# Latent attention of a two-block transformer kernel: units of one head or of two

## Chip, cores and metric

One core of a Trainium2 chip. The metric is the time of one execution on the device in microseconds (us).

## The reference, cut to what matters

The program computes two blocks of two layers each on 512 tokens of width 1024 (and 256 context tokens in the first block). The change lies in the second layer of the first block, in its latent attention: four heads, each with a nope part of 128 dimensions and a rotated part of 64; the rotated key is one for all heads. 512 queries attend to 768 keys (512 tokens and 256 of context), with values of 128 dimensions a head:

```python
q_nope, q_pe = q[..., :C_NOPE_DIM], q[..., C_NOPE_DIM:]      # 128 and 64
k_nope, v = kv[..., :C_NOPE_DIM], kv[..., C_NOPE_DIM:]       # 128 and 128
q = jnp.concatenate([q_nope, q_pe], axis=-1)
k = jnp.concatenate([k_nope, jnp.broadcast_to(k_pe, (B, T, C_HEADS, C_ROPE_DIM))], axis=-1)
...
s = jnp.einsum('bqhd,bkhd->bhqk', q, k).astype(jnp.float32) * (q.shape[-1] ** -0.5)
p = jax.nn.softmax(s, axis=-1).astype(v.dtype)
return jnp.einsum('bhqk,bkhe->bqhe', p, v)
```

## The kernel before, in words

The whole program is one kernel with five instruction streams, one for each engine, written out in program order; semaphores order them against each other. There are six attention stages (A, B in the first layer; M, the latent one, and N in the second; S and D in the second block), and all go through the same functions. All matrices of the attention are float32, and a float32 matmul shows as two records in the trace.

**Units and turns.** `units_m` (L612) makes the work of stage M as units: one head and 128 queries, so 4 heads x 4 = 16 units. `seated` (L508) puts them into turns, here one unit a turn, and gives each its places: the PSUM banks of its scores (L519), the column of its probabilities in SBUF, and its blocks of 128 keys, in groups of four, for the transposes.

```python
U["sb"] = [0, 2] if wide_s and nh == 2 else [alt, 2 + alt] if nh == 2 else [2 * alt]
```

`wide_s` is true for over 512 keys: the scores of a head then take two banks. A single head of 768 keys stands in banks 0 and 1 or in 2 and 3, by turns (`alt`). Two heads of 768 keys, as in stages B and N, take banks 0 to 3 in every turn.

**One step of the stage** (`attention`, L1146 for PE, L1875 for ACT, L2583 for DVE): in step i PE makes the scores of turn i, then the transposes ("flips") of the probabilities of turn i - 2 (`LAG`, L538), then the value products of turn i - 3. In the same step DVE takes the maxima of turn i (`maxima`, L2510: a reduce over 768 columns in PSUM and a small negation for each head) and divides the probabilities of turn i - 1 by their sum (`weigh`, L2543). ACT copies the first two groups of transposes of turn i - 2 to SBUF, makes the first exp of turn i (`exps`, L1845, which reads the scores in PSUM), copies the third group if there is one, and makes the second exp if there is one.

**Banks.** `take_bank` (L889) makes PE wait, before it writes to a bank, until the last reader has emptied it: for scores without a mask that is the exp. In `scores` (L1064) it is called for the banks of all heads of the unit before the first matmul. `next_bank` (L877) goes round a set of banks; for the transposes of stage M that set is banks 4 and 5 (`FLIP_BANKS`, L736: `"M": [4, 5], "N": [4, 5, 7]`), and such a bank is emptied by ACT's copy. The outputs of stage M stand in bank 6 (even heads) and 7 (odd heads), and `take_out` (L2604) multiplies them with their gate on DVE when a head's four units are done.

**Rotated part.** Two heads share one tile of rotated queries: one on partitions 0 to 63, one on 64 to 127; the rotated keys stand on both halves. A unit of one head uses all 128 rows in both its matmuls: POOL copies the rotated queries of the head into a buffer whose other half is zero (`QZ_at`, L533, three places in `EXQ`; the copies at L3353 to L3362), and PE waits for that copy before the rotated matmul. In stages B and N a unit is a pair of heads, and each head's matmul uses 64 rows of the array.

**Modulation steps.** The scale, shift and gate vectors of later layers are made beside everything else, in steps (`ada_step`: L903, L1758, L2365, L3185, L3514), which all engines count alike: a "chunk" (DVE multiplies a loaded 128x1024 piece by the condition, two instructions), a "sum", and an "apply" (PE transposes or multiplies the sums; DVE or ACT takes the result). A group is four chunks, a sum and an apply. `ada(n)` makes up to n steps and ends early at a "sum". `STEP_TURNS` (L289) says after which steps of stage M one such call is made: 18 calls. SyncE issues the load of a piece when DVE is done with the piece two before it (`NADA`, L18).

The projections ahead of stage M and behind it are matmuls on PE; the one behind it starts without a barrier on PE.

Of the kernel before, what the change touches and what calls it, by code (L numbers as in the profile page):

```python
# [288 lines left out]
STEP_TURNS = {"M": range(18)}  # L289
# [8 lines left out]
def program(nc, A, out_d):  # L298
    ctx = ExitStack()
    with ctx:  # L300
# [232 lines left out]
        def QZ_at(u, hf):  # L533
            return EXQ[:, u % 3 * 256 + hf * 128:u % 3 * 256 + hf * 128 + 128]

# [74 lines left out]
        def units_m():  # L612
            units = []
            for h in range(4):
                ob = 6 + h % 2
                for n in range(4):
                    heads = [[(k0, w, [(qn(h, n * 128, n * 128 + 128), kn(h, k0, k0 + w)), (None, kr(k0, k0 + w))])
                              for k0, w in ((0, 512), (512, 256))]]
                    pv = [(0, z * 128, 128, Bg(vm + z * 512 + h * 128, vm + z * 512 + (h + 1) * 128),
                           bank(ob, n * 128, n * 128 + 128)) for z in range(6)]  # L620
                    units.append(dict(heads=heads, halves=[h % 2],
                                      q=[half(qr(h // 2, n * 128, n * 128 + 128), h % 2)],
                                      nk=768, masks=[None], scale=192.0 ** -0.5, pv=pv, ob=ob, first=True, last=True,
                                      done=(h, 0, 512) if n == 3 else None))
            return seated([[U] for U in units], "M")
# [246 lines left out]
        def tensor(pe):  # L872
# [191 lines left out]
            def scores(tag, u, U):  # L1064
# [9 lines left out]
                for z in range(len(U["heads"][0])):  # L1074
                    for h in range(nh):
                        col, w, pairs = U["heads"][h][z]
                        at = U["sb"][h] * 512 + col
                        for j, (l, r) in enumerate(pairs):
                            if l is None and nh == 1:
                                pe.wait_ge(pool_value, ("qz", tag, u))  # L1080
                                l = QZ_at(u, U["halves"][h])
                            elif l is None:
                                l, r = U["q"][h], half(r, U["halves"][h])
                            pe.matmul(PS[:, at:at + w], l, r, j == 0, j == len(pairs) - 1)
                        if z == len(U["heads"][0]) - 1:
                            pe.then_inc(pe_scores, ("scores", tag, u, h))
# [15 lines left out]
            def products(tag, u, U):  # L1102
# [5 lines left out]
                if U["first"]:  # L1108
                    take_bank(U["ob"], [])
# [2732 lines left out]
```

## Time and profile before

| | |
|---|---|
| Median of 3 runs | 2261.98 us |
| The three runs | 2262.75, 2252.33, 2261.98 us |
| The profiled execution | 2252.27 us |
| Its span in the profile | 2250.5 us |
| Mean granted clock of TensorE | 0.995 |
| TensorE busy | 2187.8 us |
| VectorE busy | 1260.9 us |
| ScalarE busy | 841.0 us |
| GpSimd busy | 345.8 us |

Times in the rows are microseconds from the start of the span. A timeline row gives start and length, the engine (PE is TensorE's matmuls, PEld its weight loads, DVE VectorE, ACT ScalarE, POOL GpSimd, SP SyncE), the line of the kernel, the instruction with output and inputs, how many instructions are merged in the row, and in brackets how long the engine was idle before it and who released it. Most lines named are those of small helpers that record every instruction, so the tiles tell more than the line. The ends of matmuls are modelled and overlap the next one's start; starts are the better guide. The granted clock is a share of 2.4 GHz.

### The profile page before, as it was taken

The numbers are of one execution on the slowest core, as the hardware profiler recorded it, in microseconds if no ns is written. First come the engines' busy times: TensorE is split into PE (matmuls) and PEld (weight loads), VectorE is DVE, ScalarE is ACT, GpSimd is POOL, SyncE is SP. The second block draws the span as 40 slices with busy tenths as digits, with TensorE's granted clock in tenths as the row PEclk, the third lists the DMA queues.
The fourth block names the chain that finished last, engine by engine and source line by source line (L and its number), as shares of the span: only waits on it lengthen the run. The fifth ranks groups of instructions, "written<-read, shape, count | busy, mean of one in ns | idle before, by whom it ended". The sixth has DMA issues, their size and how long they took to land.

```text
span 2250.5 us, 30697 instructions
## 1 busy us (share of the span) xinstructions
PE 2187.8 (97%) x12072; PEld 1726.4 (77%) x12072; DVE 1260.9 (56%) x2566; ACT 841.0 (37%) x1763; POOL 345.8 (15%) x342
## 2 busy tenths in 40 slices
PE   7999999999999999999999999999999999999998
PEld 4877886688547576788777988887778688888886
DVE  3666666763346436578666565562468836433334
ACT  4366424521123105533475322223533733222243
POOL 2300211000000102030100100004533001000144
PEclk9999999999999999999999999999999999999999
DMA  8201340013233452032210455553222104322231
GB/s 322 85 20 39 111 142 1 19 57 108 84 131 104 127 177 76 11 127 93 94 39 2 140 195 189 185 188 114 88 91 78 36 1 142 129 103 94 94 107 71
DMA packets 58268, 225.85 MB, mean 100 GB/s; under 512 B 20478, under 2 KB 21118, under 8 KB 41740
## 3 DMA queue, kind: packets, MB, share of 16 engines
q1 hardware_dynamic: 58124, 223.88, 29.1%
q8 instruction: 96, 1.57, 0.3%
q14 instruction: 48, 0.39, 0.1%
HBM read 221.76 MB, written 2.10 MB: 99 GB/s over the span
## 4 chain that ended last, share of the span: by engine, by line
PE 84%; DVE 6%; ACT 2%; POOL 2%; issue 1%; DMA 0%; POOLq 0%; DVEq 0%; ACTq 0%
PE PS L86 79%; PE PS L91 5%; POOL WKr L103 1%; ACT WK L98 1%; DVE ACC L115 1%; DVE WK L108 1%; ACT WK L96 1%; ACT WKr L96 1%; DVE SM L135 0%; DVE RINGr L103 0%; DVE WK L142 0%; DVE WK L115 0%; ACT GB L96 0%; DVE X L115 0%; DVE WK L103 0%
## 5 line engine op out<-in xcount | busy, mean ns | idle before, releaser
L86 PE MATMUL PS<-Hr,RINGr 128*128 128x512 f32 (+1 forms) x1304 | 474.1, 368 | 0.0
L86 PE MATMUL PS<-Hr,GBr 128*128 128x512 f32 (+2 forms) x1396 | 462.9, 382 | 0.2 <-DVE GB L115 0.2
L96 ACT ACTIVATE WK<-PS 128x512 f32<-128x512 f32 (+3 forms) x367 | 186.0, 541 | 396.1 <-PE PS L86 224.4
L86 PEld LDWEIGHTS PS<-Hr,GBr 128*128 128x128 f32 (+1 forms) x1396 | 259.8, 188 | 52.6 <-issue 4.1
L86 PEld LDWEIGHTS PS<-Hr,RINGr 128*128 128x128 f32 x1304 | 244.8, 188 | 41.6
L103 DVE TENSOR_TENSOR RINGr<-RING,GBr 128x1024 fp32r<-128x1024 f32 x148 | 184.0, 1281 | 140.7 <-ACT GBr L96 139.9
L86 PE MATMUL PS<-RING,GB 128*128 128x256 f32 x1152 | 251.1, 379 | 0.0
L86 PEld LDWEIGHTS PS<-RING,GB 128*128 128x128 f32 x1152 | 218.2, 190 | 31.2 <-issue 2.1
L115 DVE SCALAR_TENSOR_TENSOR ACC<-ADA,SM,ACC 128x512 f32<-128x512 f32 x280 | 214.7, 788 | 47.8 <-DMA ADA<-in_l_mod 35.1
L86 PE MATMUL PS<-GBr,WKr 128*128 128x512 f32 (+1 forms) x748 | 238.4, 381 | 2.8 <-POOL WKr L103 2.8
L96 ACT ACTIVATE GBr<-RING 128x1024 fp32r<-128x1024 f32 x158 | 158.2, 1046 | 189.4 <-PE PS L86 189.4
L86 PE MATMUL PS<-H,RING 128*128 128x512 f32 (+1 forms) x544 | 204.7, 530 | 1.4 <-DVE GB L115 1.4
L96 ACT ACTIVATE GB<-PS 32x512 f32<-32x512 f32 (+3 forms) x152 | 81.0, 533 | 259.3 <-PE PS L86 253.7
L86 PE MATMUL PS<-GB 64*128 64x256 f32 (+5 forms) x976 | 166.8, 436 | 10.2 <-ACT WK L98 4.6
L86 PE MATMUL PS<-Xr,GBr 128*128 128x512 f32 (+2 forms) x484 | 175.3, 376 | 0.0
L86 PEld LDWEIGHTS PS<-H,RING 128*128 128x128 f32 x544 | 101.3, 190 | 88.4 <-issue 82.7
L86 PEld LDWEIGHTS PS<-GBr,WKr 128*128 128x128 f32 x748 | 140.6, 188 | 35.6 <-issue 7.2
L91 PE MATMUL PS<-CN,WK 128*128 128x128 f32 x1104 | 149.1, 278 | 17.4 <-DVE WK L108 9.9
L91 PEld LDWEIGHTS PS<-CN,WK 128*128 128x128 f32 x1104 | 120.6, 140 | 58.3 <-issue 40.2
L103 POOL TENSOR_TENSOR WKr<-GB,WKr 128x512 fp32r<-128x512 f32 x76 | 109.4, 1440 | 339.1 <-ACT WKr L96 336.2
L86 PE MATMUL PS<-WK,GB 128*64 128x128 f32 (+1 forms) x1856 | 148.1, 278 | 1.3 <-DVE GB L115 0.8
L98 ACT ACTIVATE WK<-WK,SM 128x128 f32<-128x128 f32 (+5 forms) x224 | 135.4, 612 | 21.3 <-DVE SM L142 13.2
(236 smaller groups left out, 3014.7 us busy)
## 6 DMA issues: line engine op xcount, KB each, us to landing
ADA<-in_l_mod SPq DMA_DIRECT2D x96, 512.0 KB, 4.2
RING<-in_l_gu SPq DMA_DIRECT2D x44, 1024.0 KB, 4.9
RING<-in_l_wd SPq DMA_DIRECT2D x24, 1024.0 KB, 5.0
RING<-in_ev_in SPq DMA_DIRECT2D x13, 1024.0 KB, 5.9
ADA<-in_od_ada SPq DMA_DIRECT2D x24, 512.0 KB, 3.7
RING<-in_od_in SPq DMA_DIRECT2D x11, 1024.0 KB, 5.9
RING<-in_l_in SPq DMA_DIRECT2D x10, 1024.0 KB, 5.0
RING<-in_l_out SPq DMA_DIRECT2D x8, 1024.0 KB, 4.9
```

What stands on the lines that cost most here:

```text
L86: self.last = self.eng.matmul(out, lhsT, rhs, start=start, stop=stop, skip_group_check=True)
L91: self.last = self.eng.transpose(out, in_, ident)
L96: self.last = self.eng.activation(out, in_, func, bias=bias, scale=scale)
L98: self.last = self.eng.activation(out, in_, func, bias=bias, scale=scale, accum_out=accum)
L103: self.last = self.eng.tensor_tensor(out, a, b, op)
L108: self.last = self.eng.tensor_scalar(out, a, s1, None, op0)
L115: self.last = self.eng.scalar_tensor_tensor(out=out, in0=a, scalar=s, in1=b, op0=op0, op1=op1)
```

## The change

A unit of stage M becomes two heads and 128 queries: eight units and eight turns. For each piece of keys PE makes the nope matmuls of both heads, then the two rotated matmuls, each on its own half of 64 rows and into its head's banks. The zero-widened queries go, with POOL's copies and its memset of their buffer. A unit's 12 blocks of keys make three groups of transposes. The outputs of both heads are taken together, in banks 6 and 7, and taken out one after the other on DVE when the pair's four units are done. The modulation calls of the stage become nine calls of up to two steps. The bank set of the transposes stays as it is. The diff:

```diff
--- before.py
+++ after.py
@@ -286,7 +286,7 @@
 
 
 
-STEP_TURNS = {"M": range(18)}
+STEP_TURNS = {"M": range(9)}
 FFN_STEPS = {"l0f": 3, "l1f": 1}
 OUT_STEPS = (3, 2, 1, 0)
 
@@ -529,11 +529,6 @@
                 for z, U in enumerate(turn):
                     U["groups"], U["bank_full"] = groups, units.index(turn[z + (len(turn) - 1 - z) // 2 * 2])
             return units, [[units.index(U) for U in turn] for turn in turns]
-
-        def QZ_at(u, hf):
-            return EXQ[:, u % 3 * 256 + hf * 128:u % 3 * 256 + hf * 128 + 128]
-
-
 
         LAG = 2
 
@@ -611,17 +606,16 @@
 
         def units_m():
             units = []
-            for h in range(4):
-                ob = 6 + h % 2
+            for t in range(2):
                 for n in range(4):
-                    heads = [[(k0, w, [(qn(h, n * 128, n * 128 + 128), kn(h, k0, k0 + w)), (None, kr(k0, k0 + w))])
-                              for k0, w in ((0, 512), (512, 256))]]
-                    pv = [(0, z * 128, 128, Bg(vm + z * 512 + h * 128, vm + z * 512 + (h + 1) * 128),
-                           bank(ob, n * 128, n * 128 + 128)) for z in range(6)]
-                    units.append(dict(heads=heads, halves=[h % 2],
-                                      q=[half(qr(h // 2, n * 128, n * 128 + 128), h % 2)],
-                                      nk=768, masks=[None], scale=192.0 ** -0.5, pv=pv, ob=ob, first=True, last=True,
-                                      done=(h, 0, 512) if n == 3 else None))
+                    s = slice(n * 128, n * 128 + 128)
+                    heads = [[(k0, w, [(qn(2 * t + h, s.start, s.stop), kn(2 * t + h, k0, k0 + w)), (None, kr(k0, k0 + w))])
+                              for k0, w in ((0, 512), (512, 256))] for h in range(2)]
+                    pv = [(h, z * 128, 128, Bg(vm + z * 512 + (2 * t + h) * 128, vm + z * 512 + (2 * t + h + 1) * 128),
+                           bank(6 + h, s.start, s.stop)) for h in range(2) for z in range(6)]
+                    units.append(dict(heads=heads, halves=[0, 1], q=[half(qr(t, s.start, s.stop), h) for h in range(2)],
+                                      nk=768, masks=[None] * 2, scale=192.0 ** -0.5, pv=pv, ob=6, both=True, first=True,
+                                      last=True, done=(2 * t, 0, 512) if n == 3 else None))
             return seated([[U] for U in units], "M")
 
         def EX(h):
@@ -1072,18 +1066,16 @@
                         else:
                             take_bank(U["sb"][h] + d, [by])
                 for z in range(len(U["heads"][0])):
-                    for h in range(nh):
-                        col, w, pairs = U["heads"][h][z]
-                        at = U["sb"][h] * 512 + col
-                        for j, (l, r) in enumerate(pairs):
-                            if l is None and nh == 1:
-                                pe.wait_ge(pool_value, ("qz", tag, u))
-                                l = QZ_at(u, U["halves"][h])
-                            elif l is None:
+                    terms = len(U["heads"][0][z][2])
+                    for j in range(terms):
+                        for h in range(nh):
+                            col, w, pairs = U["heads"][h][z]
+                            at, (l, r) = U["sb"][h] * 512 + col, pairs[j]
+                            if l is None:
                                 l, r = U["q"][h], half(r, U["halves"][h])
-                            pe.matmul(PS[:, at:at + w], l, r, j == 0, j == len(pairs) - 1)
-                        if z == len(U["heads"][0]) - 1:
-                            pe.then_inc(pe_scores, ("scores", tag, u, h))
+                            pe.matmul(PS[:, at:at + w], l, r, j == 0, j == terms - 1)
+                            if z == len(U["heads"][0]) - 1 and j == terms - 1:
+                                pe.then_inc(pe_scores, ("scores", tag, u, h))
 
             def turned(tag, at):
                 units = UNITS[tag]
@@ -1105,8 +1097,8 @@
                     by.setdefault(z[0], []).append(i)
                 lists = list(by.values())
                 order = [i for k in range(max(map(len, lists))) for l in lists for i in l[k:k + 1]]
-                if U["first"]:
-                    take_bank(U["ob"], [])
+                for b in (U["ob"], U["ob"] + 1)[0:1 + ("both" in U)] if U["first"] else ():
+                    take_bank(b, [])
                 begun = set()
                 for z, i in enumerate(order):
                     h, col, kw, V, O = blocks[i]
@@ -1115,8 +1107,8 @@
                               U["last"] and i == by[h][-1])
                     begun.add(h)
                 pe.then_inc(pe_attended, ("attended", tag, u))
-                if U["done"]:
-                    emptied[U["ob"]] = [attended_by(tag, u, U)]
+                for b in (U["ob"], U["ob"] + 1)[0:1 + ("both" in U)] if U["done"] else ():
+                    emptied[b] = [attended_by(tag, u, U)]
 
             def gate_part(t, part):
                 i, (s0, n) = fill_chunk(t), ALLT[part // 4]
@@ -1164,7 +1156,7 @@
                         for t, part in FILL["B"].get(i, ()):
                             gate_part(t, part)
                     if i in STEP_TURNS.get(tag, ()):
-                        ada(1)
+                        ada(2)
                     if behind is not None:
                         behind(i)
                 banks_from(0)
@@ -1187,7 +1179,8 @@
 
             def outputs(tags, lru=False):
 
-                by = {U["done"][0]: attended_by(tag, u, U) for tag in tags for u, U in enumerate(UNITS[tag]) if U["done"]}
+                by = {U["done"][0] + z: attended_by(tag, u, U) for tag in tags for u, U in enumerate(UNITS[tag]) if U["done"]
+                      for z in range(1 + ("both" in U))}
 
                 def ready(k, t):
                     if lru and k < 4:
@@ -1892,7 +1885,7 @@
                         if units[u]["done"] and done is not None:
                             done(tag, u, units[u])
                     if i in STEP_TURNS.get(tag, ()):
-                        ada(1)
+                        ada(2)
 
             def take_out(tag, u, U):
 
@@ -2599,7 +2592,7 @@
                         if units[u]["done"]:
                             take_out(tag, u, units[u])
                     if i in STEP_TURNS.get(tag, ()):
-                        ada(1)
+                        ada(2)
 
             def take_out(tag, u, U):
 
@@ -2607,14 +2600,15 @@
                     return
                 t, s0, s1 = U["done"]
                 dve.wait_ge(pe_attended, ("attended", tag, u))
-                g, o = Gt(t, s0, s1), bank(U["ob"], 0, s1 - s0)
-                if tag in ("S", "D"):
-                    dve.tensor_copy(g, o)
-                else:
-                    if tag == "A":
-                        own(("e", "ga", t, s0))
-                    dve.scalar_tensor_tensor(g, o, 0.5, g, ALU.mult, ALU.mult)
-                dve.then_inc(dve_value, ("o", tag, u))
+                for z in range(1 + ("both" in U)):
+                    g, o = Gt(t + z, s0, s1), bank(U["ob"] + z, 0, s1 - s0)
+                    if tag in ("S", "D"):
+                        dve.tensor_copy(g, o)
+                    else:
+                        if tag == "A":
+                            own(("e", "ga", t, s0))
+                        dve.scalar_tensor_tensor(g, o, 0.5, g, ALU.mult, ALU.mult)
+                    dve.then_inc(dve_value, ("o", tag, u))
 
             cn_keys = []
 
@@ -3335,8 +3329,6 @@
 
             close(of_pool, "norm od")
             since(pool, "norm od")
-            own()
-            pool.memset(EXQ[:, 0:768], 0.0).then_inc(pool_value)
             n = len(B_DONE)
             power("cq", n, 4)
             rope("kr", 0)
@@ -3350,16 +3342,8 @@
             for t in range(4, 7):
                 ada(4)
             since(pool, "proj M")
-            for u in STEP_TURNS["M"]:
-                ada(1)
-                if u >= len(UNITS["M"]):
-                    continue
-                U = UNITS["M"][u]
-                own()
-                if u > 2:
-                    pool.wait_ge(pe_scores, ("scores", "M", u - 3, 0))
-                hf = U["halves"][0]
-                pool.tensor_copy(half(QZ_at(u, hf), hf), U["q"][0]).then_inc(pool_value, ("qz", "M", u))
+            for _ in STEP_TURNS["M"]:
+                ada(2)
             close(of_pool, "att M")
 
 
@@ -3602,7 +3586,7 @@
                 for j in range(steps):
                     ada(4)
             for _ in STEP_TURNS["M"]:
-                ada(1)
+                ada(2)
             for j in range(4):
                 for h in (2 * j, 2 * j + 1):
                     ada(4)
```

## Rows read from the trace of the kernel before

**Rows 1.** The page, busy time by engine.

```profile
PE 2187.8 (97%) x12072; PEld 1726.4 (77%) x12072; DVE 1260.9 (56%) x2566; ACT 841.0 (37%) x1763; POOL 345.8 (15%) x342
```

**Rows 2.** Busy time by stretch: PE, PEld, DVE, ACT, POOL, clock, DMA share, GB/s.

```profile
684.00:742.50 58.50, 58.49 (x323) 43.60 (x324) 35.15 (x68) 22.28 (x50) 3.51 (x12) 1.00 0.24 73
```

**Rows 3.** Timeline, stage M's first score and the next projection's first matmul.

```profile
673.01 1.12 PE L86 MATMUL PS<-GB 128*128 128x512 f32 x2
...
750.13 10.04 PE L86 MATMUL PS<-H,RING 128*128 128x512 f32 x23
```

**Rows 4.** Timeline of one turn of stage M: start, length, engine, instruction.

```profile
687.84 1.02 PE L86 MATMUL PS<-GB 128*128 128x512 f32 x2
...
690.42 0.82 PE L91 MATMUL PS<-CN,WK 128*128 128x128 f32 x6
...
690.69 0.96 DVE L137 TENSOR_REDUCE SM<-PS 128x1 f32<-128x768 f32 x1 [1.26 <-PE PS L86]
...
691.07 1.50 PE L86 MATMUL PS<-WK,GB 128*128 128x128 f32 x12
...
691.11 0.87 ACT L96 ACTIVATE WK<-PS 128x512 f32<-128x512 f32 x2 [2.83 <-PE PS L91]
...
691.68 0.15 DVE L108 TENSOR_SCALAR SM<-SM 128x1 f32<-128x1 f32 x1
...
691.87 0.90 ACT L98 ACTIVATE WK<-PS,SM 128x768 f32<-128x768 f32 x1
...
691.94 0.62 DVE L108 TENSOR_SCALAR WK<-WK,SM 128x768 f32<-128x768 f32 x1
...
692.41 1.02 PE L86 MATMUL PS<-GB 128*128 128x512 f32 x2
...
692.48 1.53 DVE L115 SCALAR_TENSOR_TENSOR ACC<-ADA,SM,ACC 128x512 f32<-128x512 f32 x2
...
692.67 0.20 ACT L98 ACTIVATION_READ_ACCUMULATOR WK<-PS,SM 128x1 f32 x1
```

**Rows 5.** Timeline, PE's modulation work inside stage M.

```profile
682.34 0.63 PE L91 MATMUL PS<-CN,ACC 128*128 128x128 f32 x4 [0.56 <-ACT WK L96]
...
739.04 1.02 PE L86 MATMUL PS<-ACC,CN 128*128 128x512 f32 x2
```

**Rows 6.** Timeline of stage B: projection, paired scores, transposes, maxima.

```profile
428.88 1.88 PE L86 MATMUL PS<-H,RING 128*128 128x512 f32 x4
...
430.69 1.56 PE L86 MATMUL PS<-GB 64*128 64x512 f32 x8
...
432.18 0.44 PE L91 MATMUL PS<-CN,WK 128*128 128x128 f32 x2
...
432.35 1.82 DVE L135 TENSOR_REDUCE SM<-PS 128x1 f32<-128x768 f32 x2 [3.21 <-PE PS L86]
```

**Rows 7.** Timeline of stage N: transposes, ACT's third flip copy, end of second exp.

```profile
885.97 1.53 PE L91 MATMUL PS<-CN,WK 128*128 128x128 f32 x12
...
888.61 0.60 ACT L96 ACTIVATE WK<-PS 128x512 f32<-128x512 f32 x1
...
889.91 0.21 ACT L98 ACTIVATION_READ_ACCUMULATOR WK<-WK,SM 128x1 f32 x1
```

**Rows 8.** Timeline of stage M's start: an exp's read-out, the scores that waited.

```profile
678.03 0.19 ACT L98 ACTIVATION_READ_ACCUMULATOR WK<-PS,SM 128x1 f32 x1
...
678.28 1.12 PE L86 MATMUL PS<-GB 128*128 128x512 f32 x2
```

**Rows 9.** Timeline rows after PE waits, and stretches with the clock as in rows 2.

```profile
339.44 2.93 PE L86 MATMUL PS<-GB 64*128 64x512 f32 x8 [2.33 <-ACT WK L98]
...
97.16 2.08 PE L86 MATMUL PS<-GB 64*128 64x256 f32 x12 [1.39 <-POOL RINGr L103]
...
340.00:342.00 2.00, 2.00 (x8) 0.73 (x4) 1.93 (x3) 0.00 (x0) 1.62 (x1) 0.50 0.00 0
...
104.00:106.00 2.00, 2.00 (x13) 1.71 (x14) 0.00 (x0) 0.28 (x1) 0.00 (x0) 0.50 0.00 0
```

## The prediction

> **What bounds the kernel now.** I read the page's busy table first: TensorE (PE) is busy 97% of a span of 2250.5 us [rows 1]. Then the busy time by stretch over the middle of the latent attention: PE busy 58.49 of 58.50 us, at a granted clock of 1.00 (the 2.4 GHz level), while DVE has 35.15 and ACT 22.28 [rows 2]. So the stage is PE-bound, and any PE time taken away or any PE wait put in counts in full, because the projections on both sides are PE work too. The stage runs from 673.01, its first score, to 750.13, the first matmul of the next projection: 77.1 us [rows 3].
>
> The timeline of one turn [rows 4] gives the unit prices. A unit's scores start at 687.84 and its successor's transposes at 690.42: 2.58 us for four matmuls over 512 and 256 keys (each is two records), of which nope and rotated part take half each, 1.29. Six transposes: 690.42 to 691.07, 0.65. Six value products: 691.07 to 692.41, 1.34. Sum 4.57 us a turn, sixteen turns 73.1. The other 4.0 are PE's work for the modulation rows, 0.44 and twice 0.86 [rows 5], 2.2 together, and some 1.8 us of waits at the start and the end (banks, the widened queries, the first copies).
>
> **The change, part by part.**
>
> *Scores, removed.* A turn now scores two heads. Nope part 2 x 1.29 = 2.58. The two rotated matmuls stand side by side on 64 rows each. The nearest row is stage B's: its paired 64-row scores over the same 512 and 256 keys start at 430.69 and transposes follow at 432.18 [rows 6]: 1.49 us for two heads, so 1.28 for one head's time and 0.21 for leaving the two-half shape. Entering it: four full records of 0.43 start at 428.88 and would be over at 430.60; the pair starts at 430.69, so 0.09. The new order enters and leaves twice a turn (once per key piece), 0.60. Scores: 2.58 + 1.29 + 0.60 = 4.47 us against 5.16 for two turns before. 8 x 0.69 = **-5.5 us**. If entering cost nothing between matmuls of one bank it would be -10.3; if the halves did not overlap, +4.8 over before.
> The Trainium skill's TensorEngine Tiling (Array Packing), Theoretical Speedup, gives up to 2x for a contraction of 64 or less; by that the term would be -10.3 us. The same page's Key Properties say that changing the mode drains the engine. The row has both: 1.49 against 2.58.
>
> *Queries.* Sixteen POOL copies and a memset go. They hold PE only at the start; that is in the 1.8 us above. ADA steps: 18 single calls become 9 double ones. A call ends at a "sum", so both ways the stage starts at a fourth chunk and ends after three chunks of the third group; DMA loads, bias loads and PE, DVE and ACT parts stay the same in number. DVE has per turn two maxima (1.06 each: 0.99 to the negation and its issue), two weighings of 0.62 and two chunks of 1.53 [rows 4]: 6.4 of a turn of about 8.9, so it keeps up. Each chunk is loaded a turn ahead.
>
> *Transposes, added wait.* Twelve blocks in three groups, but the stage has two flip banks (4, 5), since 6 and 7 hold the outputs. The third group waits until ACT has copied the first. ACT starts that copy 0.69 after the first transpose [rows 4], a copy takes 0.60 [rows 7], hand-off 0.07: 1.36. PE has its eight transposes issued at 0.87. **0.49 us a turn, +3.9 us.** Behind it on PE stand the products and the next scores. Bounds 0.4 and 0.6.
>
> *Scores, added wait.* A single head of 768 keys had two alternating bank pairs. A pair of heads takes banks 0-1 and 2-3 every turn, and scores(i+1) waits for both exps of turn i. From the first transpose after the scores, T: maxima start at T + 0.17 (432.35 against 432.18, [rows 6]); the second starts 1.06 later; from maximum to exp is 1.18; exp with its read-out 1.00 [rows 4]; hand-off 0.05 [rows 8]. Banks free at T + 3.46. Later turns have ACT's three flip copies between the exps: stage N, with the same order on ACT, ends its second exp's read-out at 890.12 (889.91 and 0.21) with transposes from 885.97, so T + 4.15, less 0.08 for exps of 0.90 instead of 0.94, plus 0.05: T + 4.12 [rows 7]. In the steady state PE has 1.31 + 0.49 + 2.68 = 4.48 us of work there, so the wait is covered, by 0.36 us. At the ramp it is not: turn 0 and turn 1 have no transposes or products behind them (3.46 us of wait each), turn 2 has only transposes, 1.80, and waits 2.3. **+9.2 us.** One modulation transpose of 0.44 falls into these waits: -0.4. The old start and end waits, 1.8, go.
>
> *End.* The last turns hold twice the work with the same probabilities due; weighing of turn 7 ends some 6 us after its scores, PE comes to it after 9, so nothing is added. The take-out of two heads adds 0.7 us on DVE that no one waits for, as the next projection starts in other banks.
>
> Sum at full clock: -5.5 + 3.9 + 9.2 - 0.4 - 1.8 = **+5.4 us**.
>
> *The clock.* Rows of idle PE: in stage B's start PE waits 2.3 us before 339.44, and then the clock stands at 0.50 (1.2 GHz) over 340 to 342; the paired scores take 2.93 instead of 1.5. Before 97.16 PE had waited only 1.39, and the clock is at 0.50 still at 104 to 106 [rows 9]. So waits of 3.46 very likely bring the lower level. The price of one fall by the stage B row is about 1.4 for 1.5 us of work; over scores of 4.47 us I take 1.7, between 0 and 4.5. For two falls **+3.4**.
> The Trainium skill's TensorE: Matmul & The Clock Gate, Part 1, says that the engine's default is the throttled clock and idleness brings it back; that speaks for a fall after both long waits.
>
> Total +8.8 us. The profiled execution took 2252.27, so it gives 2261.1. The median of the runs shown is 2261.98, 9.7 above it (2252.33, 2261.98, 2262.75): the same kernel has two levels 0.4% apart. Against the median: **2270.8 us**.
>
> **Rivals.**
> (a) The clock stays up: +5.4, 2267.4. For it: the waits are broken by 4.5 us of dense work each time, while stage B's start had short pieces of work. Against it: the fall after a wait of 1.39. Chance 0.12.
> (b) The clock stays low over most of the start: it falls a third time before turn 3, or stays down as it did up to 106 us. Then the 13.4 us of scores and 1.8 of transposes at the start take twice as long. +10.5 to +20, 2272.5 to 2282. It decides once more than two falls are paid. This is the one that ends on the slower side. Chance 0.30.
> (c) The waits are smaller than worked out (PE finds banks free earlier, or ACT's order lets the second exp go first): 0 to +4, 2262 to 2266. Against it: the waits stand ahead of the first matmul for both heads. Chance 0.10.
> (d) Full gain, no shape price and no waits: -10.3 - 1.8 = -12, 2250. Against it: stage B and the banks. Chance 0.05.
> (e) The change doesn't do what it says: the halves run one after the other, +5.4 + 10.3 and the clock, 2281. Against it stands 1.49. Chance 0.03.
> The forecast, +5.4 with one to three falls, has 0.40.
>
> **Numbers.** A measurement of this kernel tells about 0.5%, 11.3 us, from no change. (d) is faster: 0.05. Slower: (e), most of (b), and a part for the two levels of the runs: 0.32. Same: 0.63. The range reaches from 2256 (the lower level with (c)) to 2281.
>
> **What would show it.** In the new profile: scores of a turn 4.4 to 4.6 us from first score to first transpose; PE waits of about 3.5, 3.5 and 2.3 us released by ACT's exp before the second, third and fourth turn; 0.5 us before the last four transposes of each turn; turns of about 8.95; granted clock below 1.00 in the first 25 us of the stage; stage length near 86 us. A stage under 78 us, or no PE wait at the start, would make the prediction wrong.

## The result, and the profile after

The changed kernel is a little slower: 2265.78 us against 2253.67 (medians of 20 runs each), ratio 1.0051, 95% interval 1.0034 to 1.0069, so 11.5 us, between 7.7 and 15.6. The forecast was 8.8 us more; 2270.8 was worked out against the median of the first three runs, 8.3 above that of twenty. The profiled execution has a span of 2263.4 us, 12.9 more than before's: 11.6 of it lie in stage M, as the timeline shows, 1.5 behind it; what those 1.5 are was not looked into.

The page of the changed kernel, busy time by engine:

```profile
PE 2189.6 (97%) x12072; PEld 1719.4 (76%) x12072; DVE 1261.9 (56%) x2558; ACT 839.8 (37%) x1755; POOL 339.6 (15%) x325
```

PE has the same number of records as in [rows 1] and 1.8 us more of busy time; the sixteen query copies and the memset of POOL are gone. By these totals the change would pass for nothing.

The timeline of the changed kernel: start, length, engine, instruction, merged records, the idle time before:

```profile
672.88 4.74 PE L86 MATMUL PS<-GB 128*128 128x512 f32 x16
...
677.72 0.96 DVE L137 TENSOR_REDUCE SM<-PS 128x1 f32<-128x768 f32 x1 [2.83 <-PE PS L86]
...
678.78 0.95 DVE L137 TENSOR_REDUCE SM<-PS 128x1 f32<-128x768 f32 x1
678.98 0.90 ACT L98 ACTIVATE WK<-PS,SM 128x768 f32<-128x768 f32 x1 [5.52 <-DVE SM L108]
...
679.95 0.90 ACT L98 ACTIVATE WK<-PS,SM 128x768 f32<-128x768 f32 x1
...
681.09 7.52 PE L86 MATMUL PS<-GB 128*128 128x512 f32 x16 [3.47 <-ACT WK L98]
...
688.54 0.66 PE L91 MATMUL PS<-CN,ACC 128*128 128x128 f32 x4
...
692.01 4.71 PE L86 MATMUL PS<-GB 128*128 128x512 f32 x16 [2.81 <-ACT WK L98]
...
700.82 6.29 PE L86 MATMUL PS<-GB 128*128 128x512 f32 x16 [2.17 <-ACT WK L98]
...
711.56 4.63 PE L86 MATMUL PS<-GB 128*128 128x512 f32 x16
...
716.12 1.09 PE L91 MATMUL PS<-CN,WK 128*128 128x128 f32 x8
...
717.53 0.65 PE L91 MATMUL PS<-CN,WK 128*128 128x128 f32 x4 [0.31 <-ACT WK L96]
...
718.02 2.84 PE L86 MATMUL PS<-WK,GB 128*128 128x128 f32 x24
...
720.70 1.02 PE L86 MATMUL PS<-ACC,CN 128*128 128x512 f32 x2
...
730.71 4.63 PE L86 MATMUL PS<-GB 128*128 128x512 f32 x16
739.85 4.63 PE L86 MATMUL PS<-GB 128*128 128x512 f32 x16
...
749.85 0.60 PE L91 MATMUL PS<-CN,WK 128*128 128x128 f32 x4
750.70 1.16 PE L91 MATMUL PS<-CN,WK 128*128 128x128 f32 x8 [0.25 <-ACT GATE L96]
...
761.57 13.90 PE L86 MATMUL PS<-H,RING 128*128 128x512 f32 x32
```

Four things are to be seen. The stage now runs from 672.88 to 761.57, 88.7 us against 77.1 [rows 3]. A steady turn, 730.71 to 739.85, is 9.14 us: scores 4.56 (711.56 to 716.12), transposes with their wait 1.90 (to 718.02), products 2.68 (to 720.70). Two turns of before were 2 x 4.57 [rows 4]: **in the steady state nothing is gained.** PE waits 3.47, 2.81 and 2.17 us at the start, each time for an exp. The rows before 681.09 show the chain: two maxima on DVE one behind the other, two exps on ACT one behind the other, then the banks. And the same sixteen score records take 7.52 us in turn 1, 4.71 in turn 2, 6.29 in turn 3.

The last is the clock. Busy time by stretch of the changed kernel, columns as in [rows 2] (the clock is the third figure from the end):

```profile
680.00:682.00 2.00, 0.91 (x1) 0.50 (x2) 1.35 (x2) 0.94 (x2) 0.00 (x0) 0.53 0.00 0
682.00:684.00 2.00, 2.00 (x4) 0.68 (x2) 0.00 (x0) 0.00 (x0) 0.00 (x0) 0.50 0.76 205
...
686.00:688.00 2.00, 2.00 (x8) 0.84 (x6) 0.00 (x0) 0.00 (x0) 0.00 (x0) 0.77 0.00 0
...
692.00:694.00 2.00, 1.99 (x6) 0.76 (x7) 1.90 (x6) 0.00 (x0) 0.00 (x0) 1.00 0.04 8
...
702.00:704.00 2.00, 2.00 (x4) 0.48 (x2) 1.35 (x2) 0.00 (x0) 0.00 (x0) 0.50 0.60 137
704.00:706.00 2.00, 2.00 (x8) 0.91 (x8) 0.00 (x0) 0.00 (x0) 0.00 (x0) 1.00 0.80 209
```

After the first wait the clock stands at 0.50 (1.2 GHz) from 682 to past 686, after the third from 702 to 704; after the second it does not fall (1.00 from 692 on). Against the 4.71 of turn 2, the falls cost 2.8 + 1.6 = 4.4 us.

### The profile page after: what moved, and what is told of

Same layout as the page of the kernel before. It is cut to its first block, busy times and chain, and to the rows that moved or that the text cites. A ratio compares the mean times of both kernels' runs of the same rounds, so it can differ in the third digit from the quotient of the medians.

```text
span 2263.4 us, 30642 instructions
## 1 busy us (share of the span) xinstructions
PE 2189.6 (97%) x12072; PEld 1719.4 (76%) x12072; DVE 1261.9 (56%) x2558; ACT 839.8 (37%) x1755; POOL 339.6 (15%) x325
## 4 chain that ended last, share of the span: by engine, by line
PE 84%; DVE 6%; ACT 3%; POOL 2%; issue 1%; DMA 0%; POOLq 0%; DVEq 0%; ACTq 0%
PE PS L86 79%; PE PS L91 5%; POOL WKr L103 1%; ACT WK L98 1%; DVE ACC L115 1%; DVE WK L108 1%; ACT WK L96 1%; ACT WKr L96 1%; DVE SM L135 0%; DVE RINGr L103 0%; DVE WK L142 0%; DVE WK L115 0%; ACT GB L96 0%; DVE X L115 0%; DVE WK L103 0%
## 5 line engine op out<-in xcount | busy, mean ns | idle before, releaser
L96 ACT ACTIVATE WK<-PS 128x512 f32<-128x512 f32 (+2 forms) x359 | 185.6, 550 | 396.2 <-PE PS L86 224.4
L86 PE MATMUL PS<-GB 64*128 64x256 f32 (+5 forms) x1040 | 182.3, 448 | 18.7 <-ACT WK L98 13.1
L86 PEld LDWEIGHTS PS<-GB 64*128 64x128 f32 (+1 forms) x1040 | 90.9, 192 | 86.2 <-issue 55.3
```

The lines of the kernel that those rows point to most:

```text
L86: self.last = self.eng.matmul(out, lhsT, rhs, start=start, stop=stop, skip_group_check=True)
L96: self.last = self.eng.activation(out, in_, func, bias=bias, scale=scale)
```

## The experiments

**Theory 1**: the paired scores gain less than their matmuls, because the array changes its shape in every turn; a bank wait of the transposes stands in every turn; three bank waits stand at the start, and the clock falls behind some of them. **Rival 1**: the slow scores at the start are not the clock but something of the first turns (cold weights, transfers). **Rival 2**: the halves do not overlap. Each stage below is the time from the first score to the next projection's first matmul, without the time of a gate projection that a version moves into it (7.1 us; 13.9 for two). A "fall" is a drop of the granted clock to 0.50. The column "falls" has what the slowed scores (or a slowed moved projection) lose against undisturbed ones of the same kind (4.71, with one round of halves 4.31, and the like), and the turns in which that happened. "Order" is the order of experiments 4 and 5, "one round" that of experiment 3.

| kernel | stage | falls (turns) | stage without falls | steady turn |
|---|---|---|---|---|
| before | 77.1 | 0 | 77.1 | 2 x 4.57 |
| the change | 88.7 | 4.4 (1, 3) | 84.3 | 9.14 |
| the change again | 87.5 | 3.2 (1, 3) | 84.3 | 9.14 |
| dummy matmuls | 84.3 | 0 | 84.3 | 9.14 |
| ACT order | 88.2 | 4.4 (1, 3) | 83.8 | 9.14 |
| one round | 84.5 | 3.4 (2, 3) | 81.1 | 8.75 |
| order | 85.8 | 4.8 (1, 2, 3) | 81.0 | 8.61 |
| order, one round | 79.6 | 1.7 (2) | 77.9 | 8.21 |
| the same, projection 7 moved | 76.1 | 1.7 (3) | 74.4 | 8.21 |
| gates 6, 7 moved | 80.9 | 3.3 (0, 3) | 77.6, and 3.75 of wait ahead | 9.14 |
| the same, with order, one round | 73.7 | 2.5 (0) | 71.2, and 3.78 of wait ahead | 8.21 |
| gates and their step moved | 88.8 | 4.4 (projection, 3) | 84.4 | 9.14 |
| the same, with order, one round | 82.4 | 4.1 (projection, 3) | 78.3 | 8.21 |
| one head after the other | 116.3 | 15.8 (1, 2, 3) | 100.5 | 11.20 |

In the last row the slowed transposes are not in the falls, so that 100.5 is too high as a stage at full clock. Each stage is read from one execution. Of the whole kernel experiments 1 to 4, 8 and 10 have one execution each: 2265.87, 2288.26, 2263.23, 2275.93, 2264.67 and 2263.09 us. The first four ran beside a single execution of the kernel before, 2248.12. Such single times decide nothing here, as the last section shows. Ratios below are those of the kernels that ran twelve times.

**1. Keeping PE busy through the first waits.** Dummy matmuls whose output nothing reads:

```diff
+                    if tag == "M" and i < 2:
+                        take_bank(4, [])
+                        for _ in range(3):
+                            pe.matmul(bank(4), qn(0, 0, 128), kn(0, 0, 512), True, True)
                     flips = turned(tag, i - LAG) if 0 <= i - LAG < n else iter(())
```

> The changed kernel with three matmuls more (128x512, nobody reads them) on TensorE after the scores of turns 0 and 1, that is 2.6 us of work inside the waits of 3.47 us. Stage length (first score to the first matmul of the next projection) is 88.7 us in the changed kernel. If the clock fell because TensorE stood idle: scores of turn 1 take 4.6 instead of 7.5, the waits stay (the work only fills them), the stage is 85 to 86 us, and 84 if the third fall goes too. If the slow scores had another cause (row halves, banks, DMA): still 7.5, stage 88.7.

The timeline of this kernel, PE's score rows of turns 0 to 3 and the next projection:

```profile
677.77 7.51 PE L86 MATMUL PS<-GB 128*128 128x512 f32 x22
...
685.98 7.48 PE L86 MATMUL PS<-GB 128*128 128x512 f32 x22 [0.70 <-ACT WK L98]
...
694.09 4.71 PE L86 MATMUL PS<-GB 128*128 128x512 f32 x16 [0.19 <-ACT WK L98]
...
702.90 4.71 PE L86 MATMUL PS<-GB 128*128 128x512 f32 x16 [2.17 <-ACT WK L98]
...
762.07 13.90 PE L86 MATMUL PS<-H,RING 128*128 128x512 f32 x32
```

The scores of turns 0 and 1 stay 8.21 us apart (677.77 to 685.98, as 672.88 to 681.09), so the dummies (the six records more of the x22) only fill the wait. The scores of turns 2 and 3 take 4.71, and the stage is 84.3, 4.4 less: what the falls cost in the change. Even the scores of turn 3 keep full speed behind an unfilled wait of 2.17. Rival 1 is refuted by this together with experiments 3 and 12: there the scores of turn 1 run at full speed (4.31 us) behind the same wait of 3.47 without any dummies, so the first turns are not slow as such. For the same reason this one execution doesn't show that it was the dummies that kept the clock up.

**2. One head after the other**, so that no two 64-row matmuls stand side by side:

```diff
-                    for j in range(terms):
-                        for h in range(nh):
+                    for h in range(nh):
+                        for j in range(terms):
```

> The changed kernel with the score loop's heads outside: nope and rotated part of head 0, then of head 1, so that no two halves stand side by side. If pairing the halves is what saved time in the scores (one head's 1.29 us a turn, less 0.3 for each entry and exit): scores from 4.56 to about 6.45 us, turn 11.0, stage about 104. If the halves did not overlap in the changed kernel: scores 4.6 to 5.2, stage 89 to 93.

Steady scores are 6.62 us (4.56) and the turn 11.20 (9.14), and rival 2 is refuted. Of the 2.06 us a turn the overlap of the halves is only a part: this order also goes into the 64-row shape and out of it four times a turn, not twice. With the 0.39 of experiment 3 for each further time the sum comes out, 4.56 + 1.29 + 2 x 0.39 = 6.63. The size of the loss at the start was not foreseen. Timeline and stretches of this kernel:

```profile
677.88 10.77 PE L86 MATMUL PS<-GB 128*128 128x512 f32 x16 [2.35 <-ACT WK L98]
691.01 12.65 PE L86 MATMUL PS<-GB 128*128 128x512 f32 x16 [1.31 <-ACT WK L98]
708.59 12.65 PE L86 MATMUL PS<-GB 128*128 128x512 f32 x16 [2.08 <-ACT WK L98]
726.75 6.70 PE L86 MATMUL PS<-GB 128*128 128x512 f32 x16
```

```profile
680.00:690.00 10.00, 9.70 (x17) 3.68 (x16) 2.35 (x6) 1.12 (x3) 0.16 (x1) 0.50 0.09 36
690.00:704.00 14.00, 12.99 (x18) 4.41 (x19) 5.06 (x10) 0.86 (x2) 0.37 (x1) 0.50 0.14 39
704.00:722.00 18.00, 15.92 (x32) 6.69 (x31) 6.80 (x12) 3.44 (x7) 0.00 (x0) 0.50 0.18 58
```

For 42 us the clock stays at 0.50 though PE is busy for 38.6 of them (9.70 + 12.99 + 15.92): rival (b) of the prediction, in another kernel. Its first three waits (2.35, 1.31 and 2.08) are shorter than those of the change, its price is over three times as high. The fall even came after the wait: PE works again from 677.88 on, and over 678 to 680 the granted clock was still 0.97. The same order of matmuls runs at full clock from 726.75 on (6.70), so it is not the order alone.

**3. One round of the halves**: all nope matmuls of both key pieces first, then all rotated ones, so the array goes into the two-half shape and out of it once a turn, not twice:

```diff
-                for z in range(len(U["heads"][0])):
-                    terms = len(U["heads"][0][z][2])
-                    for j in range(terms):
+                terms, nz = len(U["heads"][0][0][2]), len(U["heads"][0])
+                for j in range(terms):
+                    for z in range(nz):
...
```

> The changed kernel with all four nope matmuls of a turn before all four rotated ones, so that the 64-row shape is entered and left once a turn, not twice. If a round costs 0.30 us: scores 4.26 instead of 4.56, turn 8.84, stage 86.3. If the shape's change costs nothing between matmuls of one bank: 4.56 and 88.7.

```profile
729.24 4.24 PE L86 MATMUL PS<-GB 128*128 128x512 f32 x16
733.41 1.09 PE L91 MATMUL PS<-CN,WK 128*128 128x128 f32 x8
...
737.99 1.45 PE L86 MATMUL PS<-GB 128*128 128x512 f32 x3
```

In its timeline above, scores take 4.17 (729.24 to 733.41) and the turn 8.75 (to 737.99). So the second way in and out of the two-half shape costs 0.39 us, where the prediction had 0.30; eight give 3.1, and the stage without falls is 3.2 shorter. The way in and out that is left costs 0.30, if the bare matmuls take 3.87 as in the prediction.

**4 and 5. The wait of the third group.** First ACT alone (second exp ahead of the third copy), then with it PE's value products between the second and the third group of transposes:

```diff
+                    if tag == "M":
+                        for u, h in mine[1:]:
+                            exps(tag, u, units[u], (h,))
                     if 0 <= i - LAG < n:
                         turned(tag, i - LAG, slice(2, None))
-                    for u, h in mine[1:]:
+                    for u, h in mine[1:] if tag != "M" else ():
...
@@ PE, second run only, as it acts in stage M
-                    for _ in flips:
-                        pass
                     for u in turn_of(tag, i - LAG - 1):
                         products(tag, u, units[u])
+                    for _ in flips:
+                        pass
```

> The changed kernel with ScalarE's order alone changed: second exp before the copy of the third group of transposes. If the third group's wait on TensorE is on the copy of the first group (the bank), and ScalarE's chain is hidden behind it: steady turn still 9.14 us, only the wait before the scores of turn 3 shrinks by about 0.5, stage 88.2. If ScalarE's chain (copies and exps) bounds the steady turn: turn 8.6, stage 85.

> The changed kernel with the value products put between the second and the third group of transposes, and ScalarE's second exp before the third copy. If the third group's wait on the first group's copy (0.54 us a turn) is what took back the gain of the scores: turn from 9.14 to about 8.6, the wait before turn 3 0.5 shorter, stage 83.5 to 84.5; against before +7, ratio about 1.003. If the turn is bound by ScalarE or VectorE: turn stays near 9.1, stage 88.

ACT's order alone leaves the turn at 9.14 and cuts only the wait before turn 3, from 2.17 to 1.69. With the products in between the turn is 8.61, so 0.53 us a turn of the third group's wait can be covered. The ratio to the kernel before is 1.0038 (1.0018 to 1.0058). In the profiled execution three falls, behind waits of 3.47, 2.81 and 1.69, take back 4.8 us, and the stage is 85.8 where 83.5 to 84.5 were expected.

**6 and 7. Filling the start with work that is there anyway**: gate projections 6 and 7, which stood ahead of the stage, behind the scores of turns 0 and 1; then with experiments 3 to 5 as well. The modulation step behind projection 6 stays where it was:

```diff
+            def late_gates(i):
+                c = FIRST["od_in2"] + 2
+                if i < 2:
+                    fm(c, 8, i, "gm", 6 + i, gated("gm", 6 + i), LOC, Ht, h_od)
+                if i == 1:
+                    chunk_done(c)
...
-            attention("M")
+            attention("M", late_gates)
...
```

> The changed kernel with the last two gate projections (13.7 us of TensorE work that stood ahead of the stage) moved behind the scores of turns 0 and 1. The stage holds that work now, so its length is compared less 13.7. If the bank waits at the start and the clock are the loss: no wait before the scores of turns 1 and 2 (6.9 us), no fall before turn 1 (2.9), perhaps none before turn 3 (1.7): stage 91 to 92.6, less 13.7 is 77 to 79 against 88.7, whole kernel 10 to 11.5 us faster than the changed one, so even with the kernel before (within 0.2%). If the waits only move to another place: 88.7 and 12 us slower than before.

> The changed kernel with all three: gate projections in the waits at the start, products between the groups and the second exp first, one entry into the 64-row shape a turn. If the parts add up: turn 8.3, stage 71 to 73 less the moved work, against 77.1 before: whole kernel 4 to 6 us faster than before, ratio 0.997 to 0.998. If a new bound shows (ScalarE's exps at about 4.1 us after the scores, VectorE's 6.4 us a turn): turn 8.5 to 9, ratio 0.999 to 1.001.

The ratios are 1.0036 (1.0017 to 1.0055) and 1.0013 (0.9991 to 1.0034). The waits before turns 1 and 2 are gone, but PE now comes to the modulation transposes 7 us earlier. The timeline of the second of these kernels:

```profile
656.95 1.54 DVE L115 SCALAR_TENSOR_TENSOR ACC<-ADA,SM,ACC 128x512 f32<-128x512 f32 x2 [1.92 <-DMA ADA<-in_l_mod]
...
659.53 1.54 DVE L115 SCALAR_TENSOR_TENSOR ACC<-ADA,SM,ACC 128x512 f32<-128x512 f32 x2 [0.44 <-DMA ADA<-in_l_mod]
...
661.12 1.12 PE L91 MATMUL PS<-CN,ACC 128*128 128x128 f32 x4 [3.78 <-DVE ACC L115]
...
662.30 6.84 PE L86 MATMUL PS<-GB 128*128 128x512 f32 x16
```

PE waits 3.78 us for a chunk of DVE. DVE's chunks had waited for their transfers, 1.92 and 0.44 us; in the change it waits as long, but behind a projection of PE. The first scores run at the low clock, 6.84 us. The stage is 73.7 us, but a wait stands ahead of it and a fall at its head: the wait had moved, not gone.

**8 and 9. That modulation step moved along** behind the scores of turn 0, on PE and DVE, alone and with everything else:

```diff
...
+                if i == 0:
+                    ada(4)
...
```

> The changed kernel with the moved projections and their modulation steps alone (scores, orders and groups as in the changed kernel). If the start's waits and falls were 10 us of the loss: stage less 13.9 of moved work is 78 to 80 us against 88.7 and 77.1, with one fall or none, at the scores of turn 3. If the waits only move: 85 or more.

> As the kernel with all three edits, but the four modulation steps that stood behind the first moved projection now stand behind it again (on TensorE after the projection in step 0, on VectorE after the maxima of turn 0), so that TensorE does not wait 3.8 us for VectorE's sums ahead of the stage. If that wait, brought in by the move alone, and the clock's fall behind it took back the gain: stage less 13.9 of moved work about 71 us against 77.1 before, no wait ahead of it, ratio to before 0.997 to 0.998. If VectorE is now late with the maxima of turn 1 (it has the steps to do first): a wait of some 3 us before the scores of turn 2, stage 74, ratio 1.000.

The timeline of the version with everything:

```profile
669.93 1.54 DVE L115 SCALAR_TENSOR_TENSOR ACC<-ADA,SM,ACC 128x512 f32<-128x512 f32 x2 [1.87 <-DMA ADA<-in_l_mod]
...
674.04 0.68 DVE L115 SCALAR_TENSOR_TENSOR GB<-GB,PS 128x512 f32<-128x512 f32 x1
...
674.77 9.50 PE L86 MATMUL PS<-H,RING 128*128 128x512 f32 x16 [6.58 <-DVE GB L115]
```

Now DVE works off the modulation chunks, waiting 1.87 us for the transfer of one and 1.11 for that of another, before it comes to the gate that empties the bank which projection 7 is to write: PE waits 6.58 us and then takes 9.50 us, partly at the low clock, instead of 7.13. Without the changes of experiments 3 to 5 the stage is 88.8 us, no gain over 88.7; with everything the ratio is 1.0016 (0.9991 to 1.0040).

**10. The change once more**, unedited, for the spread of one kernel:

> The changed kernel once more, unchanged, for the spread of one execution's stage: if the clock's falls after the waits are regular, the stage is 88.7 again within 0.5 us with the scores of turns 1 and 3 slow. If which scores are slow is a matter of chance: another pattern, the stage between 84 (no fall) and 91 us, with waits of 3.47, 3.47 and 2.17 us and a turn of 9.14 us as before.

The waits are the same to 0.01 us, and the scores of the same turns, 1 and 3, are slow, but the first fall costs 1.6 us, not 2.8.

**11 and 12. Only projection 7 moved, and none.** Both with experiments 3 to 5:

```diff
+                if i == 0:
+                    fm(c, 8, 1, "gm", 7, gated("gm", 7), LOC, Ht, h_od)
+                    chunk_done(c)
...
```

> As the run with everything at once (filled start, products ahead of the last transposes, one round of row halves), but only gate projection 7 goes behind the scores of turn 0; projection 6, with the modulation step behind it, stays where the changed kernel has it. If the new waits of the filled versions come from moving projection 6 away from its modulation step, none comes here: the stage, without the 7.1 us of the moved projection, is that of the changed kernel, 88.7, less its clock falls 4.6, the first wait 3.47, 8 rounds by 0.39 (3.1) and the third group's wait over 7 turns with the 0.48 before turn 3 (4.0) = 73.5 us, plus 0 to 3.4 for falls behind the waits of 2.8 and 1.7 that stay; ahead of it nothing is lost, so 0 to 4 us less than the kernel before, ratio 0.998 to 1.001. Rival (any projection taken from ahead of the stage uncovers a wait of DVE's modulation chain): a wait of 3 to 6 us ahead of the first scores or before the projection's bank, ratio 1.001 to 1.004.

> The same without any moved projection: products ahead of the last transposes, the scalar engine's exponentials first, one round of row halves. Steady turn 8.2 us (8.61 less 0.39), first waits 3.47, 2.8 and 1.7 stay. Stage 88.7 less 4.6, 3.1 and 4.0 = 77.0 us, plus 1.7 to 6 for two or three clock falls: 79 to 83, so 2 to 6 us over the kernel before, ratio 1.001 to 1.003. Beside the run with projection 7 moved it prices the fill alone: 3.5 us and one fall. Rival (the run's level follows the falls earlier in the program, not this stage): both kernels of this call differ from their stages' sums by more than 2 us.

Timelines of the first and the second of them, PE alone:

```profile
677.05 4.34 PE L86 MATMUL PS<-GB 128*128 128x512 f32 x16
681.32 7.13 PE L86 MATMUL PS<-H,RING 128*128 128x512 f32 x16
688.47 4.31 PE L86 MATMUL PS<-GB 128*128 128x512 f32 x16
...
696.17 4.31 PE L86 MATMUL PS<-GB 128*128 128x512 f32 x16 [2.81 <-ACT WK L98]
...
704.10 6.00 PE L86 MATMUL PS<-GB 128*128 128x512 f32 x16 [1.69 <-ACT WK L98]
...
760.25 13.90 PE L86 MATMUL PS<-H,RING 128*128 128x512 f32 x32
```

```profile
667.25 4.34 PE L86 MATMUL PS<-GB 128*128 128x512 f32 x16
675.05 4.31 PE L86 MATMUL PS<-GB 128*128 128x512 f32 x16 [3.47 <-ACT WK L98]
...
682.76 6.00 PE L86 MATMUL PS<-GB 128*128 128x512 f32 x16 [2.81 <-ACT WK L98]
...
746.84 13.90 PE L86 MATMUL PS<-H,RING 128*128 128x512 f32 x32
```

No new wait this time: projection 6 still covers the modulation transposes, and the first wait is gone. The stages without falls are 74.4 and 77.9 us, 3.5 apart, the wait of 3.47. Both are 0.9 above the sums expected, because those took 4.0 us off for the third group's wait, some seven turns of it; the new order covers it in five and before turn 3, as experiment 5 shows (5 x 0.53 + 0.48 = 3.1, where 3.3 was measured). The ratios are 1.0009 (0.9987 to 1.0031) and 1.0024 (1.0001 to 1.0048), so 2.0 and 5.4 us over the kernel before, where the profiled stages give -1.0 and +2.5. Both stand about 3 us over, inside intervals of some 5 us either way: whether more than this stage is at work is left open. The best version is level with the kernel before within this interval; none was shown to beat it.

## Why the prediction was right

**The sum.** Its sign, its mechanism and its main terms held; the forecast of +8.8 is inside the interval of 7.7 to 15.6, and the profiled stage gave 11.6. Point by point, eight turns:

- *Scores, removed*: predicted 4.47 a turn and -5.5, measured 4.56 and -4.8. Mis-sized is the price of the shape: the second round of a turn costs 0.39 (experiment 3), not 0.30. The TensorEngine Tiling (Array Packing) page of the Trainium skill lists up to 2x under Theoretical Speedup and a drain at each mode change under Key Properties. The traces agree with both: the halves overlap, and with scores of 4.56 some 0.69 us a turn is paid over the 3.87 that would do without a price.
- *Third group's wait*: predicted 0.49 a turn and +3.9. In a steady turn the transposes take 1.90 where 1.31 would do, so 0.59; in the four other steps, at the start and the end, it is 0.53 (in the last one 754.37 to 756.21, 1.84 us). Together +4.5.
- *Waits at the start*: predicted 3.46, 3.46 and 2.3, less 0.4, +8.8. From one turn's scores to the next, less 4.56 and the other work, the first three turns lose 3.65 (672.88 to 681.09), 3.11 (681.09 to 692.01, less also the fall of 2.81 and the modulation transpose of 0.44) and 2.41 (692.01 to 700.82, less also transposes of 1.31 and 0.53), so +9.2. The idle times in brackets, 3.47, 2.81 and 2.17, are shorter, because each counts from the modelled end of the work before it. All of this was worked out from rows of the kernel before, of its stages B, N and M, and is the best part of the prediction. That the wait is covered in later turns held too.
- *Old waits*: -1.8 as predicted, not measured apart. Nor was the new order of the modulation calls tried by itself.
- *End*: predicted 0, and nothing shows beside the transposes' wait. In the step at 749.85 that wait is another than worked out: the second group waits for ACT's copy of a modulation gate out of a bank that it needs.
- So at full clock -4.8 + 4.5 + 9.2 - 1.8 = +7.1, against 84.3 - 77.1 = 7.2 in the trace, where the prediction had +5.4.
- *Clock*: two falls predicted for 3.4 (1.7 each), two measured for 2.8 + 1.6 = 4.4, and 3.2 in the repetition. That there were two is in part luck: the prediction had them behind the two long waits, before turns 1 and 2, and they came before turns 1 and 3, the second behind the shortest wait; experiment 5 has three. The size was taken from a stretch of stage B's work and does not hold for each fall. The Trainium skill's TensorE: Matmul & The Clock Gate, Part 1, says that idleness brings the throttled clock back; the first wait agrees with that. That there is no fall behind 2.81 us and one behind 2.17, as the rows above show, does not follow from it.

Together 11.5, where the trace has 11.6. Apart from the step at 749.85, the waits are those worked out; the error lies in the sizes. The scores, the transposes' wait and the start are off by 0.7, 0.6 and 0.4 us, 1.7 together, and the clock by 1.0.

**The rivals.** (a), the clock stays up, is refuted for the change by its stretches at 0.50; experiment 1 shows what it would be. (b) did not happen in the change; a third fall came in experiment 5, and the low clock over most of the start in experiment 2. (c) and (d) are refuted by the waits, which came as worked out, (e) by experiment 2. The turn of 8.95 and the stage "near 86" were 9.14 and 88.7.

**Where the gain went.** Pairing the halves saves 1.29 us a turn on the rotated matmuls, since the zero-widened form used the full array already. Two rounds of shape changes take 0.69 of that back, so 0.60 was realized, and the third group's wait takes 0.59. What is left over is the start: with two heads a turn the four score banks have no second set, and PE stands through the maxima and exps of both heads. No version gave the scores or the transposes more banks, so what that would bring is not shown.

## What to carry to other kernels

Twice the work in a unit doubles the chain that must end before its banks come free: add up that reader's chain and compare it with PE's other work in a steady turn and in the first turns, where there is none. Work moved into such a hole covers it, but also took its cover from another wait in four of five versions; move only what nothing behind it leaned on (projection 7, not 6). And where a form already fills the array, halving its rows gains only what is left after the shape changes; group those into one round.

## What the runs showed of the hardware

**The same waits give different clocks.** The waits at the start are equal to 0.01 us in the change, its repetition and the one-round version, and the slow scores are those of turns 1 and 3, 1 and 3, 2 and 3; in other versions they are all three or only one (table above), at 1.5 to 2.8 us each. Nor does the length of the wait order them. Without dummies and without the version of experiment 2, a wait of 3.47 was followed by slow scores in 4 executions of 6, one of 2.81 in 3 of 7, one of 1.68 to 2.18 in 9 of 11. What decides was not found. In experiment 2 the clock stayed at 0.50 over 680 to 690 though PE was busy for 9.70 of the 10 us.

**An early fall shifts a whole run.** PE issues the same work in all kernels here up to 640 us, yet the stage starts at different times. The same stretch of experiment 11 and of experiment 12:

```profile
90.00:120.00 30.00, 28.61 (x169) 27.13 (x169) 10.28 (x31) 7.19 (x18) 4.72 (x2) 0.62 0.09 35
```

```profile
90.00:120.00 30.00, 27.57 (x259) 25.41 (x257) 14.54 (x47) 14.18 (x37) 4.80 (x3) 1.00 0.20 78
```

PE is busy for 28.6 and 27.6 us and gets through 169 and 259 records, in step with the clock of 0.62 and 1.00, after the same wait of 1.39 and 1.37 us [rows 9]. (The kernel before and the change, whose profiled executions can therefore be compared, both have 0.83 there, with 220 and 219 records.) Experiment 11 would have begun its stage at 684.2 (677.05 and the 7.1 it moved), experiment 12 at 667.3: 16.9 us apart before the changed code runs, more than the whole change costs. Most of that is this one fall: behind the wait PE starts again at 97.17 and at 97.53, and the same transposes, behind the same wait of 0.96 us, start at 152.89 and at 139.48, which is 13.8 us. So its span is 2263.7 against 2249.0 though its stage is 3.5 us shorter. Single executions of this kernel therefore decide nothing under 0.8%, the spread of the twenty of the kernel before (2245.99 to 2264.13); the lengths of turns and waits inside one trace repeat far better, to some 0.01 us.
